# Turning the attention probabilities of the first layer without TensorE: VectorE blocks and transfers inside SBUF

## The reference, cut to what matters

```python
# first layer, heads 0..7 dense (keys: 512 positions + 256 context), heads 8..15 banded
s = q @ k.T * scale            # banded: keys within 128 positions only, plus 256 context keys and a sink
p = softmax(s)                 # over the keys
out = p @ v                    # per head, 128 channels
y = concat(outA, outB) * silu(z)
# all layers
mod = silu(c) @ mod_w + mod_b  # 2048 -> 6144; split in shift, scale, gate
```

## Time and profile before

| | |
|---|---|
| runs | 2538.59, 2536.96, 2537.63 us, median 2537.63 us |
| profiled execution, first to last instruction | 2534.0 us (the page gives no other time of it) |
| TensorE busy | 2497.7 us, 99% |
| VectorE busy | 1623.8 us, 64% |
| ScalarE busy | 973.6 us, 38% |
| DMA | 390.58 MB, mean 154 GB/s |
| granted TensorE clock, mean | 0.995 |
| first and last scaling of a row of probabilities | 263.94 and 780.59 us |

### The profile page before, as it was taken

How to read it: one execution, slowest core, us unless ns; L and a number is a source line. 1 busy time by engine, 2 the same in 40 slices (tenths; PEclk the granted TensorE clock), 3 DMA queues, 4 the chain that set the end, 5 groups by cost and what they waited for, 6 DMA issues and landing times.

```text
span 2534.0 us, 30108 instructions
## 1 busy us (share of the span) xinstructions
PE 2497.7 (99%) x11975; PEld 2020.2 (80%) x11975; DVE 1623.8 (64%) x2444; ACT 973.6 (38%) x1549; POOL 110.7 (4%) x117
## 2 busy tenths in 40 slices
PE   7999999999999999999999999999999999999999
PEld 4789777777777887888888887888888787887887
DVE  4456776677776768776776768456365577656532
ACT  4232444444444333432434333445455432333421
POOL 0000000000000114000000113000000000000000
PEclk8999999999999999999999999999999999999999
DMA  9955433434433754666645754323222245532342
GB/s 350 336 193 185 127 110 121 125 125 133 132 101 136 258 180 157 208 200 211 200 162 175 249 175 158 111 76 91 80 87 84 75 151 169 175 112 89 123 154 83
DMA packets 293133, 390.58 MB, mean 154 GB/s; under 512 B 11698, under 2 KB 221234, under 8 KB 289154
## 3 DMA queue, kind: packets, MB, share of 16 engines
q1 hardware_dynamic: 287184, 355.84, 43.5%
q0 software_dynamic: 5808, 32.84, 3.5%
q10 hardware_dynamic: 2, 0.00, 0.0%
HBM read 371.85 MB, written 16.78 MB: 153 GB/s over the span
## 4 chain that ended last, share of the span: by engine, by line
PE 89%; DVE 5%; DMA 2%; ACT 2%; issue 1%; SPq 1%; POOL 0%; DVEq 0%; ACTq 0%; POOLq 0%
PE G L2151 74%; PE OB L2151 6%; PE S L2151 6%; PE TB L2154 2%; PE TB L2151 1%; DMA MRAW<-in_ev_mod_w 1%; DMA MORE<-in_ev_mod_w 1%; DVE WLO L1634 1%; DVE MACC L1640 1%; DVE TT L1634 1%; ACT PB L1445 1%; DVE SM L1862 0%; SPq L1129 0%; PE OB L2154 0%; DVE Y L1634 0%
## 5 line engine op out<-in xcount | busy, mean ns | idle before, releaser
L2151 PE MATMUL G<-HHI,WLO 128*128 128x512 f32 x2560 | 1001.0, 391 | 0.0
L2151 PE MATMUL G<-HHI,WHI 128*128 128x512 f32 x1964 | 801.8, 411 | 0.5 <-DVE CLO L1640 0.5
L2151 PE MATMUL G<-HLO,WHI 128*128 128x512 f32 x1928 | 753.2, 391 | 1.6 <-DVE HLO L1640 1.4
L2151 PEld LDWEIGHTS G<-HHI,WLO 128*128 128x128 f32 x2560 | 480.7, 188 | 104.3
L1272 ACT ACTIVATE WHI<-RAW 128x1024 fp32r<-128x1024 f32 x282 | 297.5, 1056 | 560.9 <-PE G L2151 501.6
L1634 DVE TENSOR_TENSOR WLO<-RAW,WHI 128x1024 fp32r<-128x1024 f32 x282 | 344.5, 1222 | 234.9 <-ACT WHI L1272 233.0
L2151 PEld LDWEIGHTS G<-HHI,WHI 128*128 128x128 f32 x1964 | 370.9, 189 | 80.3 <-issue 6.7
L2151 PEld LDWEIGHTS G<-HLO,WHI 128*128 128x128 f32 x1928 | 363.1, 188 | 79.7 <-issue 6.7
L1640 DVE SCALAR_TENSOR_TENSOR MACC<-MWIDE,SC,MACC 128x512 f32<-128x512 f32 x420 | 320.4, 763 | 39.2 <-DMA MWIDE<-in_w_ada 12.8
L2151 PE MATMUL G<-HHI,WHITA 128*128 128x512 f32 x536 | 215.0, 401 | 0.0
L2151 PE MATMUL G<-HLO,WHITA 128*128 128x512 f32 x536 | 209.2, 390 | 0.0
(11 more groups left out here) (347 smaller groups left out, 3060.7 us busy)
## 6 DMA issues: line engine op xcount, KB each, us to landing
RAW<-in_w_in SPq DMA_DIRECT2D x128, 512.0 KB, 3.7
MWIDE<-in_od_mod_w SPq DMA_DIRECT2D x96, 512.0 KB, 4.1
MWIDE<-in_w_ada SPq DMA_DIRECT2D x96, 512.0 KB, 4.6
RAW<-in_ev_w_in SPq DMA_DIRECT2D x80, 512.0 KB, 3.5
RAW<-in_od_w_in SPq DMA_DIRECT2D x64, 512.0 KB, 3.9
MWIDE<-in_ev_mod_w SPq DMA_DIRECT2D x32, 512.0 KB, 3.8
RAW<-in_ev_w_out SPq DMA_DIRECT2D x32, 512.0 KB, 3.3
RAW<-in_od_w_out SPq DMA_DIRECT2D x32, 512.0 KB, 3.3
```

What stands on the lines that cost most here:

```text
L2151: return e.o.matmul(o, l, r, start=start, stop=stop, skip_group_check=True)
```

## The change: what it does

- `turn` on TensorE and its copies on ScalarE are gone. After the scaling, VectorE turns the row in place in blocks of 32 by 32 (`row_end`). PB becomes one buffer for all four rows of a head, and the four rows interleave in it in runs of 32 columns (`p_rows`).
- Once per head 16 transfers from PB to PT put the blocks of 32 partitions in their place: 8 issued by SyncE, 8 by ScalarE, each of 32 partitions by 6 runs of 512 bytes (`move`). The first exponential of the next head waits until all 16 of the head before have landed. The product with the values waits for the same 16. PT then has its columns in another order, and so has the product; the gate reads them back in order.
- Rows of scores alternate between the banks of S and the banks TB and OB (`row_of`). The wait of VectorE for the exponential moves to a stage of its own one step later.
- Rows 0 to 3 of a pair stay at t = 0, 3, 6, 9; rows 4 to 7 move from 12, 15, 18, 21 to 17, 20, 23, 26 (16, 19, 22, 25 in the last pair). The transfers stand 4 steps after a head's last row, the product with the values 14 (even head), 13 (odd head) or 10 steps (head 15) after it.
- The exponential of the first two rows of a banded head is done in two instructions.
- Modulation: VectorE turns MACC in blocks of 32 by 32 and sums it to 16 columns. After four jobs 16 small copies (`mod_move`), one sum and one addition finish 16 columns of MOD. TensorE has no part in it.
- VectorE's low half of a chunk (`low`) is put one chunk later than ScalarE's high half.
- The fourth WHI buffer has one fixed place. The waits that guarded its moves between two places are gone. GpSimd's descriptor scratch shrinks to 8192 bytes.

```diff
     PR = scratch("PR", [P, 3, P], F32, 46 * K1 - 1536)
     KTA = scratch("KTA", [P, 4, 768], F32, 0)
     VV = scratch("VV", [P, 6, 512], F32, 12 * K1)
-    PB = [scratch(f"PB{i}", [P, 768], F32, 24 * K1 + i * 3 * K1) for i in range(2)]
-    PT = scratch("PT", [P, 6, SEQ], F32, 30 * K1)
-    QR = scratch("QR", [P, 2, SEQ], F32, 42 * K1)
+    PB = scratch("PB", [P, 24, P], F32, 24 * K1)
...
     RESTR = scratch("RESTR", [P, P], F32R, 50 * K1 + 512)
+    PART = scratch("PART", [P, 4, 16], F32, 56 * K1)
...
@@ -199,9 +200,8 @@
         return ctx.enter_context(nc.psum_tensor(name, [P, n], F32))
 
     G = [[bank("G0"), bank("G1")], [bank("G2"), bank("G3")]]
-    S = bank("S", 1024)
-    TB = bank("TB")
-    OB = bank("OB")
+    ST = bank("ST", 2048)
+    S, TB, OB = ST[:, 0:1024], ST[:, 1024:1536], ST[:, 1536:2048]
...
         def put(*stage):
             todo.append(stage)
@@ -386,9 +374,19 @@
             put("split", at["split"])
             at["split"] += 1
 
+        def low_next():
+            put("low", at["low"])
+            at["low"] += 1
+
         def split_ahead(i):
+            while at["low"] < at["split"]:
+                low_next()
...
@@ -569,17 +576,30 @@
                 pending.append(t)
                 yield
             reduce_pending()
+            while moved:
+                move_part()
 
         def reduce_pending():
             while pending:
                 t = pending.pop()
                 put("mod_sum", t)
-                summed.add(t)
+                if t % 4 == 3:
+                    moved.extend((t // 4, q) for q in range(4))
+
+        def move_part():
+            if moved:
+                g, q = moved.pop(0)
+                put("mod_move", g, q)
+                if q == 3:
+                    put("mod_out", g)
+                    summed.update(range(4 * g, 4 * g + 4))
 
         def need_mods(t):
             while t not in summed:
                 if pending:
                     reduce_pending()
+                elif moved:
+                    move_part()
                 else:
...
@@ -705,7 +727,6 @@
             if p == 0:
                 put("k_split", 0)
             put("q_split", 2 * p)
-            put("nr_apply", ("q", 2 * p + 1))
...
@@ -716,11 +737,12 @@
                 events.setdefault(t, []).append(stage)
 
             for n in range(8):
-                later(3 * n, "rows", n)
+                later(3 * n + (0 if n < 4 else 5 if p < 7 else 4), "rows", n)
...
@@ -729,13 +751,10 @@
                         scored.append(n)
                         put("score", h, qt)
                         put("softmax", h, qt, n)
-                        two = len(score_jobs(h, qt)[1]) > 4
-                        late = 1 if a[0] % 4 == 0 else 0
-                        later(t + 4 + late, "turn", h, qt, n, 0, not two)
-                        if two:
-                            later(t + 5 + late, "turn", h, qt, n, 1, True)
+                        later(t + 1, "row_end", h, qt, n)
                         if qt == 3:
-                            later(t + 7, "pv", h)
+                            later(t + 4, "turn", h)
+                            later(t + (10 if h == 15 else 14 - i), "pv", h)
                     elif what == "pv":
                         put("pv", *a)
                         later(t + 1, "gate", *a)
@@ -743,10 +762,12 @@
                         put(what, *a)
                 t += 1
                 yield
+                if p == 7 and t > 28 and last_y < KT - 1:
+                    put("y_split", 1, last_y, h_unit)
+                    last_y += 1
             if p == 7:
-                for k in range(12, KT):
-                    put("y_split", 1, k, h_unit)
-                    yield
...
+    def p_rows(qt, kt0, kt1):
+
+        return PB[:, 4 * kt0:4 * kt1, 32 * qt:32 * qt + 32]
+
+    def move(e, h, r):
+
+        for q in range(4):
+            src = PB[32 * q:32 * q + 32, :, :].rearrange("p (k r) n -> p k r n", r=4)
+            e.o.dma_start(PT[32 * r:32 * r + 32, :, P * q:P * q + P], src[:, :, r, :]).then_inc(
...
+                e.wait_ge(v_sm, (h, 3, "turned"))
+                if h:
+                    e.wait_ge(p_pv, h - 1)
+                for r in (0, 1):
+                    move(e, h, r)
             elif stage == "x_out":
                 q, i = a
...
+                    e.wait_ge(ptd[1], h - 1)
                 else:
                     e.wait_ge(p_gemm, (2, 1))
-                e.o.activation(PB[n % 2][:, lo:768], S[:, lo:768], ACT.Exp, bias=nm,
-                               scale=1.0 if banded(h) else q_root_of(h, qt),
-                               accum_out=SM[:, i + 1:i + 2]).then_inc(*a_exp.up((h, qt)))
+                kt0 = jobs[0][0]
+                if banded(h) and qt < 2:
+                    e.o.activation(p_rows(qt, 4, 6), by_block(row_of(qt, 512, 768)), ACT.Exp, bias=nm, scale=1.0,
+                                   accum_out=SM[:, i + 3:i + 4]).then_inc(*a_exp.up((h, qt, "far")))
+                    e.o.activation(p_rows(qt, kt0, qt + 2), by_block(row_of(qt, lo, 512)), ACT.Exp, bias=nm, scale=1.0,
+                                   accum_out=SM[:, i + 1:i + 2]).then_inc(*a_exp.up((h, qt)))
+                else:
+                    e.o.activation(p_rows(qt, kt0, 6), by_block(row_of(qt, lo, 768)), ACT.Exp, bias=nm,
+                                   scale=1.0 if banded(h) else q_root_of(h, qt),
+                                   accum_out=SM[:, i + 1:i + 2]).then_inc(*a_exp.up((h, qt)))
                 if banded(h):
                     e.wait_ge(a_exp, (h, qt))
                     af(SM[:, i + 2:i + 3], SM[:, 8 + h:9 + h], ACT.Exp, nm).then_inc(*a_exp.up((h, qt, "sink")))
             elif stage == "turn":
-                h, qt, n, part, final = a
-                bank = OB if part else TB
-                e.wait_ge(p_turn, (h, qt, part))
+                h, = a
+                e.wait_ge(v_sm, (h, 3, "turned"))
                 if h:
                     e.wait_ge(p_pv, h - 1)
-                runs = runs_of(score_jobs(h, qt)[1][4 * part:4 * part + 4])
-                for x, j, m in runs:
-                    cp(PT[:, j:j + m, qt * P:(qt + 1) * P],
-                       bank[:, x * P:(x + m) * P].rearrange("p (j n) -> p j n", j=m)).then_inc(
-                        *a_turn.up((h, qt, part)))
+                for r in (2, 3):
+                    move(e, h, r)
             elif stage == "silu_a":
                 layer, k, pair, nt, u = a
...
                         SUB).then_inc(*v_h.up(("c", k)))
-            elif stage == "split":
+            elif stage == "low":
                 i, = a
                 e.wait_ge(a_whi, i)
-                tt(WLO[i % NR][:, :, :], RAW[i % NR][:, :, :], f(whi(i)[:, :, :]), SUB).then_inc(*v_wlo.up(i))
...
                 t, = a
-                _, nb, layer, _, bias = mod_jobs[t]
-                m = MOD[:, layer, 4 * nb:4 * nb + 4]
-                e.wait_ge(p_red, t)
-                e.o.tensor_reduce(m, TB[:, :].rearrange("p (n k) -> p n k", n=4), AX_X, ADD).then_inc(*v_msum.up(t))
-                e.wait_ge(v_msum, t)
-                tt(m, m, COL[:, bias + 4 * nb:bias + 4 * nb + 4], ADD).then_inc(*v_mod.up(t))
+                e.wait_ge(v_acc, 8 * t + 7)
+                e.o.transpose(MACC[:, :], MACC[:, :]).then_inc(*v_msum.up(("turned", t)))
+                e.wait_ge(v_msum, ("turned", t))
+                e.o.tensor_reduce(PART[:, t % 4, :], MACC[:, :].rearrange("p (b j) -> p b j", j=32), AX_X,
+                                  ADD).then_inc(*v_msum.up(t))
+            elif stage == "mod_move":
+                g, q = a
+                e.wait_ge(v_msum, 4 * g + 3)
+                part = PART[32 * q:32 * q + 32, :, :].rearrange("p t (c b) -> p t c b", b=4)
+                for b in range(4):
+                    e.o.tensor_copy(QUAD[32 * b:32 * b + 32, q, :].rearrange("p (t c) -> p t c", t=4),
+                                    part[:, :, :, b]).then_inc(*v_msum.up(("quad", g)))
+            elif stage == "mod_out":
+                g, = a
+                _, nb, layer, _, bias = mod_jobs[4 * g]
+                m = MOD[:, layer, 4 * nb:4 * nb + 16]
+                e.wait_ge(v_msum, ("quad", g))
+                e.o.tensor_reduce(m, QUAD[:, :, :].rearrange("p q n -> p n q"), AX_X, ADD).then_inc(
+                    *v_msum.up(("out", g)))
+                e.wait_ge(v_msum, ("out", g))
+                tt(m, m, COL[:, bias + 4 * nb:bias + 4 * nb + 16], ADD).then_inc(*v_mod.up(4 * g + 3))
             elif stage == "nr_square":
                 sq[1] = p_stat, a[0]
             elif stage == "nr_low":
...
+                        stt(rs, rs, SM[:, i + 2:i + 3], SM[:, i + 3:i + 4], ADD, ADD).then_inc(
+                            *v_sm.up((h, qt, "total")))
+                    else:
+                        tt(rs, rs, SM[:, i + 2:i + 3], ADD).then_inc(*v_sm.up((h, qt, "total")))
                     e.wait_ge(v_sm, (h, qt, "total"))
```

(103 more changed lines are left out.)

100 lines of the change are left out of this document (60 added, 40 removed).

## The result

The changed kernel takes 2633.4 us (median of 4 runs, 2630.4 to 2635.0) against 2537.3 for the one before (4 runs): 1.0377 [1.0365, 1.0389], 96 us slower where I forecast 37 faster.

The account below looks back on a forecast made before the run. TensorE was taken as the bound, VectorE next with little room. 2534.0 - 51 (TensorE) + 4 (VectorE) + 7 (landings) + 2 (end) = 2496, plus 3.6 to the runs' median: 2500 us, -1.5%; range 2482 to 2556.

Parts of the forecast that it names:

- gets 8 issues a head at 0.47 us: Transfer issues on ScalarE: 7.5 us a pair, with ScalarE busy for 32 of 71 us, so no cost.
- PB's one buffer: Hand-overs between heads: the next head's first exponential waits for 16 transfers; +7 us after VectorE's slack.
- 10.9 us of landing: Time for a head's transfers to land, bounds 10.9 to 22.8 us; late only at four hand-overs, 2.4 us each.
- the room: Time a landing has at hand-overs: 12.6 us dense, 8.5 banded after odd heads; 17.5 and 12.1 after even ones.
- The slower rival: Transfers drain at half rate and PB's one buffer sets the pace: landing 19.8 us, 2580 us in all; chance 0.19.
- Its 2624: The slower rival's kernel time if each packet takes the mean packet's 65 ns.
- rule of 189 GB/s: Skill's rule for transfers of 32 partitions, reaching 8 of 16 ports: 8.3 us alone, 2528 us by the same steps.
- with two pairs of banks ... most of the 3.1: Score rows in the heads: most of TensorE's 3.1 us wait for an exponential goes; 2 us of waits counted.
- the waits go: VectorE's waits in the heads, 9.2 us (dense) and 9.8 (banded) for exponentials and 4.5 for weights, vanish.
- +4 us over VectorE's room: Banded pairs: VectorE fits with 0.7 us, less than its remaining small waits; four pairs go over by some 1 us each.
- 51 us forecast: TensorE: 448 turns removed at 0.11 us each, 49.3 us, taken as 49, plus 2 us of waits.
- the signs of being wrong: A banded pair over 63.6 us, TensorE waiting for PT, or low halves of weights late anywhere.

Follow-up runs that it names:

- e13: Changed kernel with one pair of banks for the scores; transfers from ScalarE and SyncE read VV, not PB, and no exponential waits for a landing: 2585.5 us.
- e9: As e7, but the 16 transfers a head read VV in place of PB and no exponential waits for a landing: 2533.3 us.
- e7: Changed kernel with score rows in one pair of banks and ScalarE's eight transfers of a head issued by GpSimd: 2582.2 us.
- e6: Changed kernel without its 256 transfers (the product reads VV in place of PT) and with all score rows in one pair of banks: 2533.0 us.
- e11: As e6, also without the 64 block turns on VectorE: 2498.3 us.
- e12: Kernel before with modulation sums on VectorE only for jobs 8 to 27, behind the heads; the first eight turned by TensorE as before: 2530.8 us.
- e4: Changed kernel with all score rows in the one pair of banks they had before; transfers and queues unchanged: 2591.5 us.

## Why the prediction was wrong

- **The step that failed**: ScalarE "gets 8 issues a head at 0.47 us", "it is busy for 32 of 71 us", "so nothing". I set a sum against a share of busy time. The issues come as one block of 5.3 to 7.2 us (median 0.64 each, 0.9 on average in the longest block), and the odd head's block stands before the next pair's high half, with VectorE and TensorE behind: 52 us where I had 0 (e13, e9). The Trainium skill, "DMA: Bandwidth & Descriptors", section "Rules for kernel authors", says that spreading DMAs over engines "only saves sequencer issue time"; here that time was the cost.
- **PB's one buffer** I priced at 7 us; alone it costs 49 (e7, e9). Both terms were mis-sized. I had 10.9 us of landing, with SyncE's issues at "nothing"; in the changed kernel it is 13.4 and 13.7 where the exponential waits for it (446.4 to 459.8, 609.4 to 623.1), in e7 10.1 to 13.8 after odd and 13.0 to 17.0 after even heads. SyncE's issues are part of it: 5 to 8 us a block, begun up to 3.5 late. And the room was smaller at all hand-overs but those from an odd head to a banded one: I had 12.6 and 8.5 us after odd heads and 17.5 and 12.1 after even ones (dense, banded); in e9 the exponential starts 8.5 to 10.0 and 9.3 to 11.5 us after the block turn. So landings are late after every even head, where the forecast had none late. The slower rival has the mechanism, but it turned on one landing of 17 us everywhere and took its price from bandwidth, which no run here prices apart from the issues. Its 2624 is near the result by luck: it holds neither the banks, nor ScalarE's block, nor more than 4 of VectorE's 35 us. By the rule of 189 GB/s cited there the transfers take 8.3 us alone, and 15.9 by the steps of that rival (estimates); the landings from 10.1 to 17.0 us neither bear it out nor refute it.
- **Shared banks**, 42 us, I had only as a gain ("with two pairs of banks ... most of the 3.1"). That the product's bank is one of them is in the changed kernel: an odd row sets `tb = ob = a_exp, (h, qt)`, and the product waits for `ob`. It was in no rival.
- **VectorE in banded pairs**: the block turn was sized right (0.98, 0.84, 0.71 us against 0.955, 0.82, 0.69), the scaling stayed 0.62, and busy time is as forecast. Wrong was that the waits go: 7.8 us of them stay in the banded pair of e6. I had +4 us over VectorE's room; it is 35 (e6, e11). Banded pairs take 66.3 to 69.6 us in e6, against 60.2.
- **Turns on TensorE**: 51 us forecast, 39 measured with the block turn out (e11). The dense pair came out as worked out (64.70 against 65.4), the banded one not (62.20 against 59.2), and MACC's turns brought about 6 of the 8.8 that 20 of 28 jobs should (e12). Smaller parts of the change (low halves of weights one chunk later, exponentials in two instructions) are in e11 too; their cost was not measured apart.
- **The clock** was in no step. Of the 133 us between forecast and result, 34 are the same matmuls at a lower clock (changed kernel against e6); they are inside the terms above.
- Sum of the errors, term by term: 42 (banks, 0 forecast) + 49 (transfers, 58 for the 7 and 2 forecast) + 31 (VectorE, 35 for 4) + 12 (turns, 39 for 51) = 134, for 133. The measured terms are differences along one row of runs (changed kernel, e4, e6, e11, before), so they add up to the 96 us by construction; what supports them apart is that banks and transfers cost nearly the same in either order.

Of the signs of being wrong one came, a banded pair over 63.6 us; TensorE waited only 1.5 us for PT, and no low half of the weights was late. Its waits in the heads were 107 us, where I had put under 15.

## To carry to other kernels

Price a DMA that an engine with other work issues as a block of its time at that place in its order, and ask what is queued behind; its busy share says nothing about it. If two causes can each hold up the same work, removing one may show little gain: free each with the other already free before judging. Where work moves from TensorE to VectorE, move only what falls outside the stretch in which VectorE's order is already full.

## What the runs showed that I had not expected

- An issue of 192 packets takes its engine 0.64 us on ScalarE, 0.57 on GpSimd (medians), and one of 32 packets still 0.61 on ScalarE; a 512 KB load takes SyncE 0.37.
- VectorE's block turn in place: 0.98 us for 768 columns, 0.84 for 640, 0.71 for 512, fp32 on 128 partitions.
- 16 transfers of 96 KB through GpSimd's queue alone land later (median 5.1 us each) than eight of them beside eight of SyncE's (3.8).
